# A two-layer hybrid diffusion step: transpositions one by one between single matmuls, instead of in blocks

## The reference, cut to what matters

```python
hm = modulate(rmsnorm(x, norm_pre_mix[l]), sh1, sc1)
rq, rk, rv, rg, nq, nk, nv = project_in(hm, w_in[l])
y, _, _ = retention_bidir(rq, rk * k_scale, rv, log_g, state_f, state_b)   # 4 heads, keys of 128, values of 256
y_ret = retention_output(y, rg, ret_gn_gain[l])
y_na = neighbourhood_attention(nq * q_scale, nk, nv, k_ctx, v_ctx, rpb)    # 8 heads of 64, window 8 x 16, softmax
mixed = (g_ret * (y_ret @ w_ret_out) + g_na * (y_na @ w_na_out)) @ w_o
x = x + g1 * rmsnorm(mixed, n_post_mix)
hf = modulate(rmsnorm(x, n_pre_ffn), sh2, sc2)
x = x + g2 * rmsnorm((silu(hf @ wg) * (hf @ wu)) @ wd, n_post_ffn)         # hidden width 2816
```

## Time and profile before

| What | Value |
|---|---|
| Median of three timed runs | 2136.46 us |
| Span of the profiled execution | 2134.6 us |
| The median over that span | 1.9 us |
| PE busy (matmuls) | 2103.7 us, 99% of the span, 14114 matmuls |
| PE busy (weight loads) | 2011.7 us, 94% |
| DVE busy | 1545.8 us, 72% |
| ACT busy | 931.8 us, 44% |
| Mean granted clock of PE | 0.998 of full |

### The profile page before, as it was taken

The page is one execution under the profiler, slowest core; times in us unless marked ns, Lnnn a source line. Parts: engine busy times, 40 slices in busy tenths (PEclk is TensorE's granted clock), DMA queues, the critical chain, the costliest instruction groups (busy, mean ns, idle before and its releaser), DMA issues.

```text
span 2134.6 us, 34256 instructions
## 1 busy us (share of the span) xinstructions
PE 2103.7 (99%) x14114; PEld 2011.7 (94%) x14114; DVE 1545.8 (72%) x2477; ACT 931.8 (44%) x1494; POOL 101.6 (5%) x195
## 2 busy tenths in 40 slices
PE   7999999999999999999999999999999999999998
PEld 6999999999989999999889999999999899999997
DVE  5688767477757887887877886755864668787786
ACT  5655432476334433332476554225753544233332
POOL 0000010110000000000000000001100000000000
PEclk9999999999999999999999999999999999999999
DMA  7333354233334222222433333532233322222223
GB/s 301 114 118 128 104 172 144 99 101 133 134 115 162 70 81 98 80 79 80 168 131 101 117 119 134 166 126 80 85 119 129 129 60 80 79 80 81 98 79 138
DMA packets 63099, 246.08 MB, mean 115 GB/s; under 512 B 7776, under 2 KB 8064, under 8 KB 60256
## 3 DMA queue, kind: packets, MB, share of 16 engines
q1 hardware_dynamic: 42336, 158.55, 21.7%
q0 software_dynamic: 20608, 85.35, 11.4%
HBM read 230.20 MB, written 13.66 MB: 114 GB/s over the span
## 4 chain that ended last, share of the span: by engine, by line
PE 91%; DVE 5%; ACT 2%; DMA 1%; issue 1%; DVEq 1%; SPq 0%; ACTq 0%
PE unit L496 11%; PE unit L497 11%; PE unit L498 11%; PE unit L508 9%; PE unit L511 9%; PE unit L509 9%; PE sc L496 4%; PE sc L497 4%; PE sc L498 4%; PE tp L496 4%; PE tp L497 4%; PE tp L498 4%; PE tp L839 1%; DVE junk L1780 1%; PE sc L815 1%
## 5 line engine op out<-in xcount | busy, mean ns | idle before, releaser
L508 PE MATMUL unit<-hmh,wh 128*128 128x320 f32 x1120 | 337.8, 309 | 1.9 <-DVE sig L2209 1.1
L509 PE MATMUL unit<-hml,wh 128*128 128x320 f32 x1120 | 337.3, 309 | 0.0
L1678 DVE TENSOR_TENSOR wl<-raw,wh 128x1024 fp32r<-128x1024 f32 x204 | 246.8, 1221 | 123.0 <-ACT wh L1184 121.0
L511 PE MATMUL unit<-hmh,wl 128*128 128x320 f32 x1120 | 255.2, 309 | 0.0
L1184 ACT ACTIVATE wh<-raw 128x1024 fp32r<-128x1024 f32 x204 | 210.1, 1050 | 95.6 <-DMA raw<-w_main 95.6
L1780 DVE CUSTOM_DVE_ANT_0 junk<-ada,csb,par 128x1024 f32<-128x1024 f32 x160 | 205.5, 1284 | 31.5 <-DMA ada<-w_ada 12.1
L508 PEld LDWEIGHTS unit<-hmh,wh 128*128 128x128 f32 x1120 | 210.2, 188 | 2.6 <-issue 2.6
L509 PEld LDWEIGHTS unit<-hml,wh 128*128 128x128 f32 x1120 | 210.3, 188 | 0.0
L496 PE MATMUL unit<-wh,hmh 128*128 128x256 f32 (+1 forms) x640 | 199.2, 311 | 1.5 <-ACT qks L1298 1.5
L497 PE MATMUL unit<-wl,hmh 128*128 128x256 f32 (+1 forms) x640 | 198.0, 309 | 0.0
L498 PE MATMUL unit<-wh,hml 128*128 128x256 f32 (+1 forms) x640 | 198.0, 309 | 0.0
(11 more groups left out here) (458 smaller groups left out, 5297.1 us busy)
## 6 DMA issues: line engine op xcount, KB each, us to landing
raw<-w_main SPq DMA_DIRECT2D x276, 512.0 KB, 4.0
ada<-w_ada POOLq DMA_DIRECT2D x80, 512.0 KB, 4.5
first<-w_first SPq DMA_DIRECT2D x8, 1024.0 KB, 19.3
x<-x_keep POOLq DMA_DIRECT2D x3, 2560.0 KB, 10.2
bias<-biases POOLq DMA_DIRECT2D x32, 192.0 KB, 2.7
x_keep<-x POOLq DMA_DIRECT2D x10, 512.0 KB, 2.9
bias<-biases POOLq DMA_DIRECT2D x16, 256.0 KB, 4.1
gains<-g_rows POOLq DMA_DIRECT2D x4, 1024.0 KB, 6.2
```

The source lines that it names most:

```text
L508: pe.matmul(u[:, h, 0:n], a[0], xs[h][0], start=f, stop=False)
L509: pe.matmul(u[:, h, 0:n], a[0], xs[h][1], start=False, stop=False)
L511: mm = pe.matmul(u[:, h, 0:n], a[1], xs[h][0], start=False, stop=z)
L1678: dve.tensor_tensor(wl[slot[i]][:, :], raw[slot[i]][:, :], f32(wh[slot[i]][:, :]), ALU.subtract)\
```

## The change

The blocks are dissolved. Helpers that issued a block become generators that issue one transposition each time they are asked, and the loops that issue matmuls ask after each single matmul (`next(turns, None)`). `product`, `linear`, `mixer_part`, `down_tile` and the filling columns take such a generator. The number of transpositions and of matmuls is the same, and so are their operands; the waits that stood ahead of a block stand ahead of its first transposition.

```diff
+    def take_next(self):
+        self.eng.wait_ge(self.free[(self.count + 1) % 2], (self.count + 1) // 2)
+        return self.tile(1)
...
-            def product(out, a, b, first, last):
+            def product(out, a, b, first, last, turns=iter(())):
+
                 pe.matmul(out, a[0], b[0], start=first, stop=False)
+                next(turns, None)
                 pe.matmul(out, a[0], b[1], start=False, stop=False)
-                return pe.matmul(out, a[1], b[0], start=False, stop=last)
+                next(turns, None)
+                mm = pe.matmul(out, a[1], b[0], start=False, stop=last)
+                next(turns, None)
+                return mm
...
+            def later(n, turns):
+                for _ in range(n):
+                    yield
+                for mm in turns:
+                    yield mm
...
                 for c in range(KD):
                     mm = pe.transpose(banks(i)[c // 4][:, c % 4 * P:(c % 4 + 1) * P], of[:, c * P:(c + 1) * P], ident[:, :])
-                mm.then_inc(tr_ready, 1)
-                tiles.add()
+                    if c == KD - 1:
+                        mm.then_inc(tr_ready, 1)
+                        tiles.add()
+                    yield
...
                         if n == 0 and k == 4:
-                            turn_tile()
-                        product(u[:, 0, 0:CUT], w(k), [t[:, k, 0:CUT] for t in (hmh, hml)], k == 0, k == KD - 1)
+                            turns = tile_turns()
+                        product(u[:, 0, 0:CUT], w(k), [t[:, k, 0:CUT] for t in (hmh, hml)], k == 0, k == KD - 1,
+                                turns if n == 0 and k >= 4 else iter(()))
...
-                    u = U.take()
+                    u = U.take_next()
                     for t in range(TILES):
                         for c in range(2):
                             out = u[:, c, t * P:(t + 1) * P] if t < 4 else sc[0][:, c * P:(c + 1) * P]
-                            mm = pe.transpose(out, y[:, t, c * P:(c + 1) * P], ident[:, :])
-                    U.give(mm)
+                            yield pe.transpose(out, y[:, t, c * P:(c + 1) * P], ident[:, :])
+
+                def column_and_head():
+
+                    turns = head_turns()
+                    column(later(6 * KD - 2 * TILES + 1, turns))
+                    for mm in turns:
+                        U.give(mm)
...
                         column()
-                        column()
-                        turn_head()
+                        column_and_head()
...
-                    if 1 <= i <= STEPS:
-                        turn(i - 1)
+                    turns = turns_of(i - 1) if 1 <= i <= STEPS else iter(())
                     due = pieces(p, j)
-                    for _ in range(due - done):
+                    for _ in range(3 * (due - done)):
                         next(source)
+                        next(turns, None)
+                    for _ in turns:
+                        pass
...
                     mixer_part(u, t, range(before))
-                    turn_tile()
-                    U.give(mixer_part(u, t, range(before, KD)))
+                    U.give(mixer_part(u, t, range(before, KD), tile_turns()))
...
                     down_tile(u, FB - 2, t, weights, True, False)
-                    if l < DEPTH - 1:
-                        turn_tile()
-                    U.give(down_tile(u, FB - 1, t, last_weights, False, True))
+                    U.give(down_tile(u, FB - 1, t, last_weights, False, True, tile_turns() if l < DEPTH - 1 else iter(())))
```

More of the change, by code:

```diff
@@ L523, in slab_over, with column @@
                 slab_done.extend([(unit_ready, U.count)] * n)
-            def column(wait_chunk=None):
+            def column(turns=iter(())):
                 w, _, _ = slab(P)
-                linear(w, (hmh, hml), KD, wait_chunk)
+                linear(w, (hmh, hml), KD, turns=turns)
                 slab_over()
@@ L766, in _ @@
                     column()
-                    column()
                     if j == 0:
-                        turn_head()
+                        column_and_head()
+                    else:
+                        column()
                     column()
@@ L792, in half_columns @@
                             for k in range(KD):
-                                mm = product(lin[:, bank, 0:HALF], w(k), [t[:, k, h * HALF:(h + 1) * HALF] for t in (hmh, hml)],
-                                             k == 0, k == KD - 1)
-                                if k == KD - 1:
-                                    mm.then_inc(lin_ready, 1)
-                                    lins.add()
-                                    if h == 1:
-                                        slab_done.append((lin_ready, lins.count))
-                                yield
+                                a, b = w(k), [t[:, k, h * HALF:(h + 1) * HALF] for t in (hmh, hml)]
+                                for n, (x, y_) in enumerate(((0, 0), (0, 1), (1, 0))):
+                                    last = k == KD - 1 and n == 2
+                                    mm = pe.matmul(lin[:, bank, 0:HALF], a[x], b[y_], start=k == 0 and n == 0, stop=last)
+                                    if last:
+                                        mm.then_inc(lin_ready, 1)
+                                        lins.add()
+                                        if h == 1:
+                                            slab_done.append((lin_ready, lins.count))
+                                    yield
                 def score(i):
@@ L827, in score, with turns_of @@
                         mm.then_inc(nsc_ready, 1)
-                def turn(i):
+                def turns_of(i):
                     j = i % 5
@@ L839, in turn @@
                             mm = pe.transpose(tp[hh][:, to * P:(to + 1) * P], s[:, hh, n * P:(n + 1) * P], ident[:, :])
-                        mm.then_inc(t_ready, 1)
+                            if n == len(tiles) - 1:
+                                mm.then_inc(t_ready, 1)
+                            yield
                 def weigh(p, group, hh):
@@ L914, in _, with mixer_part @@
                 parts = []
-                def mixer_part(u, t, ks):
+                def mixer_part(u, t, ks, turns=iter(())):
                     cols = slice(t * P, (t + 1) * P)
@@ L925, in mixer_part @@
                             mm = product(u[:, h, :], (mh[:, k, cols], ml[:, k, cols]), (hi[:, 0, ns], lo[:, 0, ns]),
-                                         k == 0, k == KD - 1)
+                                         k == 0, k == KD - 1, turns)
                         if t == TILES - 1 and k < KD - 1:
@@ L943, in _, with down_tile @@
                     mixer_part(u, t, range(before))
-                    turn_tile()
-                    U.give(mixer_part(u, t, range(before, KD)))
+                    U.give(mixer_part(u, t, range(before, KD), tile_turns()))
                 slab_over()
-                def down_tile(u, b, t, weights, first, last):
+                def down_tile(u, b, t, weights, first, last, turns=iter(())):
                     for n in range(2):
@@ L953, in down_tile @@
                             mm = product(u[:, n, :], [m[:, b % 2, k, t * P:(t + 1) * P] for m in (hidh, hidl)],
-                                         (hi[:, k, :], lo[:, k, :]), first and k == 0, last and k == 1)
+                                         (hi[:, k, :], lo[:, k, :]), first and k == 0, last and k == 1, turns)
                     return mm
```

8 lines of the change are left out of this document (5 added, 3 removed).

## The result

The changed kernel takes 2148.46 us (median of 4 runs, 2147.81 to 2149.35) against 2136.71 us of the kernel before beside it (2135.92 to 2137.36): the ratio is 1.0055 [1.0043, 1.0067], slower by 11.8 us where 2147.5 us and +11.0 were forecast. The profiled span grew from 2134.6 to 2147.5 us, by 12.9; the profiled run of the changed kernel is the slowest of its four, 0.9 over their median, and that of the kernel before is 0.25 under its own, so the spans lie further apart than the medians.

A forecast was written before the change was run, and what follows sets the result against it. PE, busy 99% of the span at full clock, was taken as the bound. Terms 1.0 + 6.9 + 2.0 + 0.3 + 0.8 = +11.0 us on the 2134.6 span gave 2145.6, timed 2147.5 us; range 2140 to 2155.

The forecast's parts named there:

- The price of a transposition: On PE: a transposition between wide matmuls costs 0.11 us, against 0.109 for one in a block.
- The term of borders: 340 new borders of transposition and wide matmul: up to 0.002 us each with 320 columns, 0.01 with 512; +1.0 us.
- The head's copy: Heads: ACT's copy loses the block as cover, so PE waits 0.86 us more at eight places; +6.9 us.
- The layer's end: Tiles there: the eighth transposition comes later, and the ACT and DVE chain that sets the pace waits; +2.0 us.
- PE's waits grow to some 5 us: Sign that the forecast is right: later tile turns, with PE's waits at the layer's end some 5 us in all.
- Behind the output products: Slack, except that the next slab's low part comes 0.1 to 0.2 us late, twice; +0.3 us.
- The attention: Dense steps keep 0.5 us of slack; the last five steps of a layer lose 0.4 us a layer; +0.8 us.

The follow-up runs named there:

- extra singles: Kernel before plus 320 unread identity transpositions in plain gate-up columns, one by one: 2171.23 us; the same in blocks of 40: 2169.9 us.
- The run with six behind: Changed kernel, but six of a head's ten transpositions stay behind the column's last matmul instead of two: 2145.33 us.
- heads-alone kernel: Kernel before with only the heads' transpositions one by one, all others in blocks: 2143.86 us (1.0031).
- four in a row: Kernel before with only the tiles' transpositions changed: a tile's first four in a row, the other four one by one: 2137.27 us (1.0002).
- the attention up to step 15: Kernel before with only the attention's transpositions one by one, up to step 15 of each layer, in blocks behind: 2138.39 us (1.0009).
- turning the order: Kernel before with only the attention's transpositions one by one, each ahead of its filling matmul instead of behind it: 2137.52 us (1.0002).
- the tiles alone: Kernel before with only the token tiles' transpositions (output product, last down product, first columns) one by one: 2139.77 us (1.0011).
- the blocks with filling matmuls in the attention: Kernel before, all blocks kept, with filling matmuls between the two heads' blocks in attention steps 18 and 20: 2134.47 us (0.999).
- The attention alone: Kernel before with only the attention's transpositions one by one, each behind its filling matmul: 2139.28 us (1.001).

## Why the prediction was right

The mechanism of the largest term was right and carries the result. That the median came within 1 us is in part luck. By the spans the forecast is 1.9 us short: the attention came dearer by 1.2, a wait that was not foreseen added 0.8, the output products were dearer by some 0.5, and the layer's end cheaper by some 0.7 (with the borders shared out).

- **The price of a transposition** held: 0.26 us a pair in the trace, extra singles 0.004 to 0.006 dearer than in a block. The term of borders was up to 0.002 with 320 columns; the heads and the attention show 0.003 (0.259 - 0.147 - 0.109). With 512 columns it was 0.01, and the output products show 0.009. The 264 borders with 320 columns should read 256 (56 in the heads, 200 in the attention), which changes nothing. The Trainium skill ("TensorE: Matmul & The Clock Gate", Part 1, the engine queue depths) lets the queue pull weight loads ahead of matmuls in flight; the runs agree with one load ahead and show none of two, so nothing was gained by it.
- **The head's copy** was the term that mattered: 0.86 forecast at each of eight places, 0.86 in the rows, 3.6 a layer with the borders. The run with six behind shows that it is the lost cover, and not the spreading by itself.
- **The layer's end** was right in mechanism (ACT waits for the eighth transposition) and too high in size: +2.0 against +1.5. I had ACT 1.1 us late at tile 1, another 0.2 to 0.3 at tile 2 and some 0.6 at tile 4. By its starts (less the 6.0 us by which PE comes to the stage later) it is late by 0.5, 1.0, 1.1, 2.3 and 1.5 us at tiles 0 to 4: a little less each time, and much of tile 3's delay is made up. That PE's waits grow to some 5 us was a poor sign: they came to 4.2 on ACT, but stand at 3.8 in the heads-alone kernel, which loses nothing there.
- **Behind the output products** the mechanism held, and two kinds of loss add up: +0.3 forecast for both layers and another 0.2 of the borders, +0.4 measured in layer 1 with the tiles one by one, in whatever company. Of that, 0.19 are 21 borders with 512 columns, 0.17 are the wait for the low part of the next slab (forecast: 0.1 to 0.2), and the rest are borders of tile 3. The wait is shorter than the list of waits counts, but the weight load at the place of the earlier trace rows shows it in the changed kernel:

```profile
654.03 0.19 PEld L501 LDWEIGHTS unit<-hmh,wh 128*128 128x128 f32 x1 [0.34 <-DVE wl L1712]
```

DVE made that part from 652.76 on, 1.8 us later than in the earlier trace rows when PE's own 5.7 are taken off. With four in a row the whole falls to 0.07. In layer 2 three kernels with the tiles one by one show 0.44 to 0.45 too; the +0.6 of the changed kernel has another 0.2 in small stalls, and a kernel with the tiles in blocks (the attention up to step 15) shows +0.9 over the same stretch, so these vary between runs.
- **The attention** is the term that was mis-sized: +0.8 and some +0.4 of the borders forecast, +2.4 measured. The dense steps had the slack that I read from the earlier trace rows: no wait appears in them. What I missed stands in the same trace: a load behind the 64-row scores finds no cover, and the change put a dearer one there. That is 0.7 us a layer, shown by turning the order; 0.2 are borders. The late steps cost 0.3 a layer, close to the +0.4 of the forecast, but not by its account alone: of the 2.0 us of waits for `tp` 1.1 are won back, and 1.0 for the scores' bank and the normalised weights come.
- **Left open**: 0.8 us of the span are a wait for a slab's low part at 532 us, behind the attention. Kernels with blocks in the attention show between nothing and 1.1 there, so I don't put it down to the change.

## What to carry over

A block of small instructions between a producer's last matmul and the next use of its buffer may be what hides the copy in between: before spreading it, look at what was running beside it, and leave behind the producer as many as the copy is long. Where another engine takes the result of the last of a series, spread only so far that the last one stays within that engine's slack (here 1.3 us behind a block's end at the one tile where it was read, and four in a row were enough). A wait that grows is not yet a loss: look at what the stage takes. Filling matmuls helped here where PE sets the pace; where ACT does, they moved the wait.

## What was not expected of the hardware

In these traces a weight load starts while the matmul before it runs, except behind the score matmuls of 64 rows: the first full-row instruction behind these pays its own load, 0.056 us for a transposition and 0.11 for a filling matmul, at all 30 places.

The other concerns the clock. Windows of the kernel before, of the one with the tiles alone and of the one with the heads alone, in this order (stretch; length, busy us of PE and the others with counts; granted clock):

```profile
1070.00:1074.00 4.00, 4.00 (x12) 3.09 (x12) 3.78 (x7) 3.97 (x10) 0.00 (x0) 0.59 0.01 2
```

```profile
1070.00:1074.00 4.00, 4.00 (x22) 3.27 (x21) 3.74 (x8) 3.66 (x9) 0.00 (x0) 1.00 0.01 2
```

```profile
1074.00:1078.00 4.00, 4.00 (x19) 3.26 (x18) 3.92 (x8) 3.97 (x10) 0.00 (x0) 1.00 0.01 2
```

Behind PE's wait of 1.93 us and the block of tile 0, the clock of the kernel before was granted at the lower of its two levels, 1.2 GHz, for most of this stretch (0.59 on average over it), and seven matmuls of 512 columns took 0.43 us each instead of 0.23. The slices of the page, 53 us long, don't show it. The kernel with the tiles alone waited 1.72 us, with wide matmuls among its transpositions, and kept 1.00. It is not the spreading that kept it: the heads alone have the same block of tile 0 there as the kernel before, waited 1.98 us ahead of it, and kept 1.00 too, and so did the blocks with filling matmuls in the attention (2.02 us). The attention alone, with that block and a wait of 1.96 us, fell as the kernel before did. What decides it isn't shown. The 1.6 us that the lower clock took cost the kernel before nothing, as ACT sets the pace there: the heads alone, without them, took 0.05 us longer over the stage.
